# The chunk-gating stage of a hybrid diffusion step: b_s as a VectorE addend, and the scan's opening inside the gating rounds

## Chip, cores and metric

The kernel runs on one core of one Trainium2 chip. The metric is the device time of one execution in microseconds. Arithmetic is f32 throughout; a product of two f32 operands takes TensorE two records in the profile, and a transpose takes one.

## What is computed

One layer for 128 context tokens and 256 latent tokens (384 columns, three tiles of 128), model width 2048. The part that matters here is the middle of `token_mix`: the gating half (`y_g`), and what the scan needs first of each head pair (decay, `a`, `kk`, `kd`).

```python
za = za + p['mu_shift'] * (shift_fn(za) - za)
r, k, v, g = (za[..., i * D_A:(i + 1) * D_A] for i in range(4))
lw = za[..., 4 * D_A:4 * D_A + 2 * LORA_W].reshape(b, t, 2, LORA_W)
la = za[..., 4 * D_A + 2 * LORA_W:].reshape(b, t, 2, LORA_A)
wl = (p['w0'] + jnp.einsum('btdr,drc->btdc', jnp.tanh(lw), p['w2'])).astype(F32)
decay = jnp.exp(-jnp.exp(-jax.nn.softplus(-wl) - 0.5))
a = jax.nn.sigmoid((p['a0'] + jnp.einsum('btdr,drc->btdc', la, p['a2'])).astype(F32))
kk = (k * p['k_k']).astype(F32).reshape(b, t, H_A, HEAD_A)
kk = kk / jnp.maximum(jnp.linalg.norm(kk, axis=-1, keepdims=True), 1e-12)
kd = k.astype(F32)[:, :, None] * (1.0 + (a - 1.0) * p['k_a'].astype(F32))
...
u = jax.nn.gelu(zb[..., :D_B])
vg = layernorm(jax.nn.gelu(zb[..., D_B:]), p['ln_v_w'], p['ln_v_b'])
vc = vg.reshape(b, t // CHUNK, CHUNK, H_B, HEAD_B)
sp = jnp.einsum('hpq,bnqhc->bnphc', p['w_s'], vc) + p['b_s'].T[:, :, None]
y_g = u * sp.reshape(b, t, D_B)
```

`b_s` has one value per head and position in the chunk (8 x 128). It is the same for all 128 channels of a head and for the three chunks.

## The kernel before

Activations lie with channels on the 128 partitions and the 384 tokens along the free dimension: `z` holds one block of 128 channels per index, PSUM (`ps`) has eight banks. The program is a row of Blocks, each with one instruction list per engine; all engines meet at the end of a Block. In front of the change lie the modulation and the input projection (until about 533 us), behind it the scan (607 to 1168 us), the output projection and the expert mixer.

**The gating Block.** It first makes statistics: means of `vg` (TensorE into bank 0, VectorE subtracts), squares of the keys summed by head (bank 6), and the variance of `vg` (bank 1), from which ScalarE and VectorE make `rstd` by a square root and a reciprocal. Then come eight rounds (HB = PAIRS = 8), one for each head of the gate and one pair of key heads. All rings have two slots (RING = 2).

- TensorE, round j: `over_heads(j)` spreads the inverse key norms over the partitions (a matmul of 16 rows and 384 columns), `turn(j)` transposes three tiles of the normalised `vg`, and `mix(j - 1)` does, for each of three tiles, a matmul of one row that puts `b_s` into the bank (row of ones times `bsp`) and then the matmul with `w_s` on top. `mix(HB - 1)` follows the last round.
- ScalarE, round j: `affine(j + 1)` (weight and bias of the layer norm, into `vn`), `copy(j)` (the transposed tiles from PSUM to `vt`).
- VectorE, round j: `scale(j + 2)` (times `rstd`), `key(j + 1)` (writes `kk`), `gate(j)` (u times the mix, read from PSUM).
- SyncE loads `w_s`, `b_s` on one partition, the spreading matrix, and three of the modulation weights that the scan uses up later (1 MB each).

**The scan Block.** It has eight head pairs, one after another. Each starts from values that its opening makes: TensorE's four `front` matmuls (64 rows, 384 columns, from `lora`, the loaded w2 and a2 of the pair), ScalarE's `front_gates` (sigmoids) and `front_factors` (exponentials), and VectorE's 18 `front_step`s (prefix sums, centring, `kd` and the products bq and kq). For pairs 1 to 7 the opening is woven into the pair before; for pair 0 it stands at the head of the Block, ahead of everything else, and SyncE's load of `lora` for it as well. After the opening, TensorE transposes bq, kq and (when POOL has copied it) `vs`, VectorE makes the kr products, TensorE makes 12 score products into PSUM and VectorE masks them (L1065). POOL's list in this Block starts with clearing and filling `c32`, two copies of identities, and then the copy of `vs`. Order on each engine is that of the program; waits are on semaphores that count instructions.

Of the kernel before, what the change touches and what calls it, by code (L numbers as in the profile page):

```python
# [23 lines left out]
ALU = mybir.AluOpType  # L24
# [3 lines left out]
P = 128  # L28
# [21 lines left out]
RING = 2  # L50
# [109 lines left out]
def build_program(nc, x_t, c_t, cols_in, tables_in, spread_in, w_ada, w_in, w2a2, w_s, b_s, state_t, w_out, w_query,  # L160
# [9 lines left out]
    with ctx:  # L170
# [419 lines left out]
        ka1 = sb(g_scope, "ka1", [P, PAIRS])  # L590
        with ExitStack() as c_scope, nc.Block() as block:
            wsp = sb(c_scope, "wsp", [P, HB, P])
            bsp = sb(c_scope, "bsp", [1, HB, P])
# [9 lines left out]
            mixed, gated = sem("mixed"), sem("gated")  # L603
# [61 lines left out]
            def _(act):  # L665
                nc.scalar.activation(z[:, Z_LW, :], z[:, Z_LW, :], ACT.Tanh)
# [87 lines left out]
        with ExitStack() as d_scope, nc.Block() as block:  # L754
# [4 lines left out]
            lora = buf("lora", [P, 2, P])  # L759
# [3 lines left out]
            sg = [buf(f"sg{d}", [P, T]) for d in range(2)]  # L763
            aa = [buf(f"aa{d}", [P, T]) for d in range(2)]
            cum = buf("cum", [P, T])
            bon = buf("bon", [P, T])
            cen = [buf(f"cen{d}", [P, T]) for d in range(2)]
            cex = [buf(f"cex{d}", [P, T]) for d in range(2)]

            fac = [[sg[0], cex[0], buf("fac0", [P, T])], [sg[1], cen[1], buf("fac1", [P, T])]]  # L770
            tot = [buf(f"tot{d}", [P, TILES]) for d in range(2)]
            half_next = [buf(f"halfnext{d}", [P, TILES]) for d in range(2)]
            half = [buf(f"half{d}", [P, TILES]) for d in range(2)]
            half2 = [buf(f"halftwo{d}", [P, 1]) for d in range(2)]
            kd = [buf(f"kd{d}", [P, T]) for d in range(2)]
            bq = aa
            kq = [fac[0][2], fac[1][2]]

# [23 lines left out]
            def signal(name, per):  # L802
                return Signal(sem(name), per)

            y_copied, state_stored = sem("y_copied"), sem("state_stored")
            lora_landed, state_landed = sem("lora_landed"), sem("state_landed")
            v_copied, gates_in, gates = signal("v_copied", 1), signal("gates_in", 4), signal("gates", 4)
            centred, factors = signal("centred", 2), signal("factors", 2)
            multiplied = signal("multiplied", 4)
# [20 lines left out]
            front_chain = sem("front_chain")  # L830

            def zb(first, it):
                return z[:, bass.ds(it + first, 1), :].rearrange("p o t -> p (o t)")

            def colr(name, it, more=0):
                return cols[:, bass.ds(it + (COLS[name][0] + more), 1)]
# [23 lines left out]
            def _(sp):  # L860
# [24 lines left out]
                load_lora(0)  # L885
# [33 lines left out]
            def _(act):  # L919
                K = EXP_HALF  # L920

                def front_gates(it, d):
                    gates_in.wait(act, it, 2 * d + 1)
                    gates.inc(nc.scalar.activation(sg[d][:, :], ps[:, 6, 0:T], ACT.Sigmoid, bias=colr("w0", it, PAIRS * d)))
                    gates_in.wait(act, it, 2 * d + 2)
                    gates.inc(nc.scalar.activation(aa[d][:, :], ps[:, 7, 0:T], ACT.Sigmoid, bias=colr("a0", it, PAIRS * d)))

                def front_factors(it, d):
                    centred.wait(act, it, d + 1)
                    srcs = ((cen[d], -K), (cex[d], -K), (cen[d], K)) if d == 0 else ((cex[d], K), (cen[d], K), (cex[d], -K))  # L930
                    for i, (src, sc) in enumerate(srcs):
                        nc.scalar.activation(fac[d][i][:, :], src[:, :], ACT.Exp, scale=sc)
                    factors.inc(nc.scalar.activation(half_next[d][:, :], tot[d][:, :], ACT.Exp, scale=-K))

# [11 lines left out]
                def one(it, more):  # L946
# [9 lines left out]
                    if more:  # L956
                        operands.wait(act, it, 2)
                        halves.wait(act, it, 2)
                        front_gates(it + 1, 0)
                    for n in range(NL * GR):  # L960
# [5 lines left out]
                        if more:  # L966
                            if n == 0:
                                front_gates(it + 1, 1)
                                nc.scalar.activation(zb(Z_G, it), zb(Z_G, it), ACT.Sigmoid)
                            elif n in (7, 11):  # L970
                                front_factors(it + 1, n // 4 - 1)
# [25 lines left out]
            def _(dve):  # L997
                FRONT = 20

                def front_step(it, n):  # L1000

                    d = n // 4 if n < 8 else (n - 8) // 5
                    fc = Chain(dve, front_chain, it, FRONT)
                    if n < 8:
                        k = n % 4
                        fc.n = 7 * d + (0, 3, 4, 7)[k]
                        if k == 0:
                            gates.wait(dve, it, 2 * d + 1)
                            if d:
                                fc.wait(7)  # L1010
                            for i in range(TILES):
                                c = slice(i * P, (i + 1) * P)
                                fc.done(nc.vector.tensor_tensor_scan(cum[:, c], table("ones"), sg[d][:, c], 0.0, ALU.mult, ALU.add))
                        elif k == 1:
                            fc.wait()
                            fc.done(nc.vector.tensor_scalar(tot[d][:, :], cum[:, P - 1:T:P], 0.5, None, ALU.mult))
                        elif k == 2:
                            fc.wait()
                            for i in range(TILES):
# [1382 lines left out]
```

## Time and profile before

| | us |
|---|---|
| median of 3 runs | 3145.44 |
| lowest and highest | 3135.82 to 3153.9 |
| the profiled execution | 3150.04 |
| its span | 3148.3 |
| TensorE busy in the span | 2918.8 |
| VectorE, ScalarE, POOL busy | 2139.9, 1203.8, 874.3 |

The profile is of one execution. PE is TensorE's matmuls and PEld its weight loads, DVE is VectorE, ACT ScalarE, POOL GpSimd, SP SyncE. A timeline row tells start, duration, engine, line, operation, output and inputs, count of merged records, and in brackets how long the engine had been idle and who released it. The whole stage that the change touches is 2.4% of the span, and the opening of pair 0 another 0.5%, so the page of totals says little of them; stretches and timelines do. Matmul records overlap, so the pace of matmuls is the distance from start to start, not the duration.

### The profile page before, as it was taken

Reading aid. Unit: us, or ns where it says so; the run is one execution under the profiler, and the core shown is the slowest. Engines: PE = TensorE matmul, PEld = TensorE weight load, DVE = VectorE, ACT = ScalarE, POOL = GpSimd, SP = SyncE. Lnnn points to the kernel's source line nnn. Section 1 sums busy time; section 2 is a strip of 40 time slices with the busy share of each in tenths; the row PEclk is TensorE's granted clock in tenths of the full one; section 3 lists DMA queues with packets and bytes.
Section 4 is the critical chain, followed back from the end, with each engine's and each line's share of the span. In section 5 each row is a group of like instructions: output and inputs, shape, how many; then the busy total and the mean of one; then the engine's idle time right before and its main releaser. Section 6 shows DMA issues by size and latency. Waiting matters only on the chain.

```text
span 3148.3 us, 62824 instructions
## 1 busy us (share of the span) xinstructions
PE 2918.8 (93%) x25976; PEld 2621.9 (83%) x25976; DVE 2139.9 (68%) x3018; ACT 1203.8 (38%) x1773; POOL 874.3 (28%) x554
## 2 busy tenths in 40 slices
PE   6899999899999999969998999999997999999997
PEld 5799998477787778959998999999996887777776
DVE  1455532455565545368994988887776999989997
ACT  2433333233333333252334555454332433333333
POOL 0000000022222211026774444331112344343431
PEclk8899999599999998979998999999998999999998
DMA  9533333033443333235566999999999999999995
GB/s 386 206 131 120 133 122 113 4 113 126 139 155 125 128 127 118 80 135 196 198 230 240 361 394 396 388 332 398 412 383 392 418 418 418 417 418 418 418 417 239
DMA packets 207556, 815.23 MB, mean 259 GB/s; under 512 B 81505, under 2 KB 101089, under 8 KB 118274
## 3 DMA queue, kind: packets, MB, share of 16 engines
q1 hardware_dynamic: 104898, 527.19, 44.9%
q0 software_dynamic: 36864, 268.45, 20.5%
q10 hardware_dynamic: 65600, 16.78, 2.4%
q8 instruction: 149, 2.44, 0.3%
q14 instruction: 45, 0.37, 0.0%
HBM read 771.98 MB, written 40.37 MB: 258 GB/s over the span
## 4 chain that ended last, share of the span: by engine, by line
PE 27%; DMA 13%; DVE 8%; issue 3%; POOL 2%; ACT 1%; another core or an unknown queue 1%; SPq 1%; DVEq 0%; ACTq 0%; POOLq 0%
DMA work<-act_table 11%; PE ps L1697 6%; PE ps L1698 6%; PE ps L1699 6%; POOL wlo L1687 2%; DVE work L2282 2%; DVE x L2187 2%; PE ps L2044 1%; PE ps L2045 1%; PE ps L2046 1%; PE ps L1951 1%; PE ps L1953 1%; PE ps L1952 1%; DVE wlo L2287 1%; PE ps L2013 1%
## 5 line engine op out<-in xcount | busy, mean ns | idle before, releaser
L1697 PE MATMUL ps<-hhi,whi 128*128 128x256 f32 x2048 | 589.1, 288 | 19.4 <-POOL wlo L1687 10.6
L1698 PE MATMUL ps<-hlo,whi 128*128 128x256 f32 x2048 | 581.7, 284 | 0.0
L1699 PE MATMUL ps<-hhi,wlo 128*128 128x256 f32 x2048 | 581.6, 284 | 0.0
L2044 PE MATMUL ps<-whi,hhi 128*128 128x512 f32 x1024 | 402.3, 393 | 33.2 <-DVE hlo L2265 18.1
L1697 PEld LDWEIGHTS ps<-hhi,whi 128*128 128x128 f32 x2048 | 395.2, 193 | 24.3 <-POOL wlo L1687 13.1
L2077 POOL DMA_INDIRECT work<-expert_v,idx x128 | 289.7, 2263 | 442.0 <-DVE work L2282 420.0
L2045 PE MATMUL ps<-wlo,hhi 128*128 128x512 f32 x1024 | 399.7, 390 | 0.0
L2046 PE MATMUL ps<-whi,hlo 128*128 128x512 f32 x1024 | 399.3, 390 | 0.0
L1698 PEld LDWEIGHTS ps<-hlo,whi 128*128 128x128 f32 x2048 | 395.4, 193 | 0.0
L1699 PEld LDWEIGHTS ps<-hhi,wlo 128*128 128x128 f32 x2048 | 395.1, 193 | 0.0
L2077 POOL DMA_INDIRECT x<-u_rows,idx x128 | 231.8, 1811 | 471.2 <-DVE x L2187 275.6
L265 PE MATMUL ps<-hhi,whi 128*128 128x384 f32 x1040 | 349.9, 336 | 5.6 <-DVE hlo L357 5.6
L266 PE MATMUL ps<-hlo,whi 128*128 128x384 f32 x1040 | 348.3, 335 | 0.0
L267 PE MATMUL ps<-hhi,wlo 128*128 128x384 f32 x1040 | 348.2, 335 | 0.0
L2282 DVE SCALAR_TENSOR_TENSOR work<-work,dots 128x2048 f32<-128x2048 f32 x127 | 297.8, 2345 | 0.1
L1687 POOL TENSOR_TENSOR wlo<-raw,whi 128x2048 fp32r<-128x2048 f32 x40 | 200.0, 5003 | 264.2 <-ACT whi L1807 171.6
L2044 PEld LDWEIGHTS ps<-whi,hhi 128*128 128x128 f32 x1024 | 192.8, 188 | 82.6 <-DVE wlo L2287 24.7
L254 DVE TENSOR_TENSOR wlo<-raw,whi 128x2048 fp32r<-128x2048 f32 x66 | 150.9, 2288 | 152.0 <-ACT whi L248 152.0
L2187 DVE SCALAR_TENSOR_TENSOR x<-x,htok 128x2048 f32<-128x2048 f32 x88 | 226.9, 2584 | 6.4 <-DMA x<-u_rows,idx 5.9
L2046 PEld LDWEIGHTS ps<-whi,hlo 128*128 128x128 f32 x1024 | 192.8, 188 | 40.5
L2045 PEld LDWEIGHTS ps<-wlo,hhi 128*128 128x128 f32 x1024 | 192.8, 188 | 39.3
L1912 ACT ACTIVATE whi<-raw 128x2048 fp32r<-128x2048 f32 x64 | 122.9, 1921 | 222.5 <-PE ps L2046 212.7
(330 smaller groups left out, 5486.9 us busy)
## 6 DMA issues: line engine op xcount, KB each, us to landing
raw<-expert_u SPq DMA_DIRECT2D x94, 1024.0 KB, 7.2
x<-w_ada SPq DMA_DIRECT2D x64, 1024.0 KB, 5.3
work<-expert_v SPq DMA_DIRECT2D x64, 1024.0 KB, 14.7
raw<-expert_v SPq DMA_DIRECT2D x64, 1024.0 KB, 14.7
raw<-w_in SPq DMA_DIRECT2D x50, 1024.0 KB, 4.8
raw_more<-expert_u SPq DMA_DIRECT2D x34, 1024.0 KB, 8.4
z<-w_ada SPq DMA_DIRECT2D x32, 1024.0 KB, 14.0
raw<-w_out SPq DMA_DIRECT2D x16, 1024.0 KB, 4.8
```

The source lines that it names most:

```text
L265: pe.matmul(bank, hi[:, k, :], hhi[:, k, :], start=(k == 0), stop=False)
L266: pe.matmul(bank, hi[:, k, :], hlo[:, k, :], start=False, stop=False)
L267: last = pe.matmul(bank, lo[:, k, :], hhi[:, k, :], start=False, stop=(k == KD - 1))
L1697: pe.matmul(bank, whi[:, r, k, :], moving_hi, start=(k == 0), stop=False)
L1698: pe.matmul(bank, whi[:, r, k, :], moving_lo, start=False, stop=False)
L1699: last = pe.matmul(bank, wlo[:, r, k, :], moving_hi, start=False, stop=(k == KD - 1))
L2044: pe.matmul(bank, ah, vh[:, part], start=first, stop=False)
L2045: done = pe.matmul(bank, ah, vl[:, part], start=False, stop=False)
L2046: done = pe.matmul(bank, al, vh[:, part], start=False, stop=last)
L2077: nc.gpsimd.indirect_dma_start(out=buf, out_offset=None, in_=rows, in_offset=bass.IndirectOffsetOnAxis(ap=idx[:, s:s + 1], axis=0)).then_i ...
L2187: nc.vector.scalar_tensor_tensor(out=ug[s % UG], in0=ug[s % UG], scalar=1.0, in1=htok[:, :], op0=ALU.mult, op1=ALU.mult, accum_out=dots[:, ...
L2282: nc.vector.scalar_tensor_tensor(out=accs[:, :], in0=vg[n], scalar=dots[:, bass.ds(it * 4 + n, 1)], in1=accs[:, :], op0=ALU.mult, op1=ALU. ...
```

## The change

- `b_s` is loaded on all 128 partitions (`bsp` is [P, HB, P]). The matmuls of one row are gone from `mix`. VectorE has a new `add_bias(j)` that reads the mix from PSUM, adds `bsp` (the same for the three tiles) and writes a new buffer `biased` (two slots); `gate(j)` reads that. The bank is given back after `add_bias`.
- The opening of pair 0 leaves the head of the scan Block. `lora` is loaded in the gating Block, behind `spread`. TensorE runs front sums 0 and 1 around `over_heads(0)`, and sums 2 and 3 in rounds 1 and 2, all in banks 0 and 1. ScalarE runs the gates of direction 0 ahead of `affine(0)`, those of direction 1 after `copy(2)`, and the factors after `copy(3)` and `copy(4)`. VectorE runs steps 0 and 1 ahead of round 0 and the others between `add_bias` and `gate` of the eight rounds.
- The buffers and the helper functions move to the scope that both Blocks share; their bodies are the same but for the banks.

```diff
+        FRONT_IN_ROUND = ((2, 3), (4, 5), (6, 7), (8, 9, 10), (11, 12), (13, 14), (15, 16), (17,))
...
+        def front_sums(pe, it, n, banks=(6, 7)):
+            if n == 0:
+                pe.wait_ge(lora_landed.sem, it * 16 + 16)
+            if n >= 2:
+                gates.wait(pe, it, n - 1)
+            r = slice(64 * (n // 2), 64 * (n // 2) + 64)
+            gates_in.inc(pe.matmul(ps[:, banks[n % 2], 0:T], lora[r, n % 2, :], z[r, (Z_LW, Z_LA)[n % 2], :], start=True, stop=True))
...
-            bsp = sb(c_scope, "bsp", [1, HB, P])
+            bsp = sb(c_scope, "bsp", [P, HB, P])
+            biased = sb(c_scope, "biased", [P, RING, T])
...
-                sp.dma_start(bsp[:, :, :], b_s).then_inc(loads.sem, 16)
+                sp.dma_start(bsp[:, :, :], b_s.to_broadcast([P, HB, P])).then_inc(loads.sem, 16)
                 sp.dma_start(spread[:, :], spread_in).then_inc(loads.sem, 16)
+                sp.dma_start(lora[:, :, :], w2a2[0]).then_inc(lora_landed.sem, 16)
...
                     if j >= RING:
-                        pe.wait_ge(gated.sem, j - RING + 1)
+                        pe.wait_ge(bias_added.sem, j - RING + 1)
                     for c in range(TILES):
-                        out = ps[:, 4 + u, c * P:(c + 1) * P]
-                        pe.matmul(out, table("ones")[0:1, :], bsp[:, j, :], start=True, stop=False)
-                        last = pe.matmul(out, vt[:, u, c * P:(c + 1) * P], wsp[:, j, :], start=False, stop=True)
+                        last = pe.matmul(ps[:, 4 + u, c * P:(c + 1) * P], vt[:, u, c * P:(c + 1) * P], wsp[:, j, :],
+                                         start=True, stop=True)
...
+                pe.wait_ge(tanh_done.sem, tanh_done.v + 1)
+                front_sums(pe, 0, 0, (0, 1))
+                over_heads(0)
+                pe.wait_ge(act_to_dve.sem, act_to_dve.v + 1)
+                front_sums(pe, 0, 1, (0, 1))
                 for j in range(HB):
-                    over_heads(j)
+                    if j:
+                        over_heads(j)
                     turn(j)
+                    if j in (1, 2):
+                        front_sums(pe, 0, j + 1, (0, 1))
                     if j:
                         mix(j - 1)
                 mix(HB - 1)
...
+                front_gates(act, 0, 0, (0, 1))
                 affine(0)
                 for j in range(HB):
                     if j + 1 < HB:
                         affine(j + 1)
                     copy(j)
+                    if j == 2:
+                        front_gates(act, 0, 1, (0, 1))
+                    if j in (3, 4):
+                        front_factors(act, 0, j - 3)
...
+                def add_bias(j):
+                    dve.wait_ge(mixed.sem, j + 1)
+                    nc.vector.tensor_tensor(biased[:, j % RING, :].rearrange("p (c t) -> p c t", c=TILES),
+                                            ps[:, 4 + j % RING, 0:T].rearrange("p (c t) -> p c t", c=TILES),
+                                            bsp[:, j:j + 1, :].to_broadcast([P, TILES, P]), ALU.add).then_inc(bias_added.sem, 1)
+
                 def gate(j):
-                    dve.wait_ge(mixed.sem, j + 1)
-                    nc.vector.tensor_tensor(z[:, Z_U + j, :], z[:, Z_U + j, :], ps[:, 4 + j % RING, 0:T], ALU.mult).then_inc(gated.sem, 1)
+                    dve.wait_ge(bias_added.sem, j + 1)
+                    nc.vector.tensor_tensor(z[:, Z_U + j, :], z[:, Z_U + j, :], biased[:, j % RING, :], ALU.mult)
 
                 scale(0)
                 scale(1)
                 key(0)
+                dve.wait_ge(loads.sem, loads.v + 48)
+                for n in range(2):
+                    front_step(dve, 0, n)
                 for j in range(HB):
                     if j + 2 < HB:
                         scale(j + 2)
                     if j + 1 < HB:
                         key(j + 1)
+                    add_bias(j)
+                    for n in FRONT_IN_ROUND[j]:
+                        front_step(dve, 0, n)
                     gate(j)
...
-                load_lora(0)
...
-                for step in (front_gates, front_factors):
-                    for d in range(2):
-                        step(0, d)
...
-                for n in range(18):
-                    front_step(0, n)
...
-                for n in range(4):
-                    front(0, n)
```

## Rows read from the trace of the kernel before

**Rows 1.** Stretches: busy us (records) of the engines, granted clock, DMA share, GB/s

```profile
core 0: us, PE busy (x) PEld busy (x) DVE busy (x) ACT busy (x) POOL busy (x), PEclk, DMA share, GB/s
...
534.00:545.00 11.00, 11.00 (x35) 4.64 (x34) 3.55 (x5) 8.99 (x14) 0.00 (x0) 1.00 0.90 324
...
549.00:556.00 7.00, 3.25 (x9) 1.29 (x7) 4.57 (x5) 2.98 (x5) 0.00 (x0) 0.84 0.00 0
...
568.00:574.00 6.00, 6.00 (x17) 3.47 (x16) 1.64 (x3) 1.20 (x2) 0.00 (x0) 0.50 0.00 0
...
608.00:620.00 12.00, 5.72 (x11) 2.65 (x11) 7.87 (x23) 7.00 (x14) 3.33 (x4) 0.50 0.09 27
```

**Rows 2.** Timeline of one gating round, TensorE

```profile
568.25 1.64 PE L643 MATMUL ps<-inv,spread 16*128 16x384 f32 x2
...
569.82 0.90 PE L635 MATMUL ps<-tab,vn 128*128 128x128 f32 x3
...
570.65 0.79 PE L653 MATMUL ps<-bsp,scan_tab 1*128 1x128 f32 x2
...
571.38 0.80 PE L654 MATMUL ps<-wsp,vt 128*128 128x128 f32 x2
...
575.00 1.64 PE L643 MATMUL ps<-inv,spread 16*128 16x384 f32 x2
```

**Rows 3.** Timeline of the entry to the rounds

```profile
549.37 0.58 ACT L675 ACTIVATE rstd<-ps,eps 128x384 f32<-128x384 f32 x1 [4.41 <-PE ps L625]
549.98 2.55 DVE L708 RECIPROCAL rstd<-rstd 128x384 f32<-128x384 f32 x1 [2.06 <-ACT rstd L675]
...
553.92 0.90 PE L635 MATMUL ps<-tab,vn 128*128 128x128 f32 x3 [3.75 <-ACT vn L681]
```

**Rows 4.** Timeline of the end of the rounds and the opening of pair 0

```profile
606.43 0.55 DVE L721 TENSOR_TENSOR z<-z,ps 128x384 f32<-128x384 f32 x1 [3.79 <-PE ps L654]
...
607.33 1.28 ACT L924 ACT_TABLE_LOAD   x1 [9.09 <-PEq L591]
...
609.41 5.24 PE L1140 MATMUL ps<-z,lora 64*128 64x384 f32 x8 [3.02 <-DMA lora<-w2a]
...
610.82 0.50 POOL L899 COPY vs<-z 128x384 f32<-128x384 f32 x1
...
611.09 0.58 ACT L924 ACTIVATE sg<-ps,cols 128x384 f32<-128x384 f32 x1 [2.48 <-PE ps L1140]
611.71 1.05 DVE L1013 TENSOR_TENSOR_SCAN cum<-scan_tab,sg 128x128 f32<-128x128 f32 x3 [4.72 <-ACT sg L924]
...
621.61 0.56 DVE L1043 TENSOR_TENSOR fac<-kd,fac 128x384 f32<-128x384 f32 x1
...
623.13 0.85 PE L1169 MATMUL ps<-tab,vs 128*128 128x128 f32 x3
...
623.91 1.23 PE L1184 MATMUL ps<-kr,aa 64*128 64x256 f32 x4
...
625.81 7.56 DVE L1065 TENSOR_TENSOR G<-ps,scan_tab 128x512 f32<-128x512 f32 x12 [0.25 <-PE ps L1184]
```

**Rows 5.** Timeline: pairs of 128-row matmuls in pair 0; 16-row matmuls in a row

```profile
678.77 0.49 PE L1285 MATMUL ps<-s,kr 128*128 128x128 f32 x2
...
679.19 0.69 PE L1289 MATMUL ps<-vtok,G 128*64 128x64 f32 x16
...
682.10 0.39 PE L1312 MATMUL ps<-vtok,btok 128*128 128x128 f32 x2
...
682.32 0.39 PE L1311 MATMUL ps<-sa,btok 128*128 128x128 f32 x2
...
1182.75 9.29 PE L1444 MATMUL ps<-inv,spread 16*128 16x384 f32 x14 [3.33 <-DVE inv L1501]
```

**Rows 6.** Groups of VectorE's instructions, 549 to 607.2 us

```profile
L716 DVE SCALAR_TENSOR_TENSOR kk<-z,cols,ps 128x384 f32<-128x384 f32 x8 | 4.9, 613 | 5.6 <-PE ps L643 5.6
L721 DVE TENSOR_TENSOR z<-z,ps 128x384 f32<-128x384 f32 x8 | 4.4, 554 | 35.7 <-PE ps L654 35.7
L712 DVE TENSOR_TENSOR z<-z,rstd 128x384 f32<-128x384 f32 x8 | 4.3, 551 | 0.0
```

More of the change, by code:

```diff
@@ L590, in build_program @@
         ka1 = sb(g_scope, "ka1", [P, PAIRS])
+        lora = sb(g_scope, "lora", [P, 2, P])
+        sg = [sb(g_scope, f"sg{d}", [P, T]) for d in range(2)]
+        aa = [sb(g_scope, f"aa{d}", [P, T]) for d in range(2)]
+        cum = sb(g_scope, "cum", [P, T])
+        cen = [sb(g_scope, f"cen{d}", [P, T]) for d in range(2)]
+        cex = [sb(g_scope, f"cex{d}", [P, T]) for d in range(2)]
+        fac = [[sg[0], cex[0], sb(g_scope, "fac0", [P, T])], [sg[1], cen[1], sb(g_scope, "fac1", [P, T])]]
@@ new lines, in build_program, with signal @@
+        tot = [sb(g_scope, f"tot{d}", [P, TILES]) for d in range(2)]
+        half_next = [sb(g_scope, f"halfnext{d}", [P, TILES]) for d in range(2)]
+        kd = [sb(g_scope, f"kd{d}", [P, T]) for d in range(2)]
+        bq = aa
+        kq = [fac[0][2], fac[1][2]]
+        def signal(name, per):
+            return Signal(sem(name), per)
+        gates_in, gates = signal("gates_in", 4), signal("gates", 4)
+        centred, factors, multiplied = signal("centred", 2), signal("factors", 2), signal("multiplied", 4)
@@ new lines, in front_gates, with front_factors @@
+        def front_gates(act, it, d, banks=(6, 7)):
+            gates_in.wait(act, it, 2 * d + 1)
+            gates.inc(nc.scalar.activation(sg[d][:, :], ps[:, banks[0], 0:T], ACT.Sigmoid, bias=colr("w0", it, PAIRS * d)))
+            gates_in.wait(act, it, 2 * d + 2)
+            gates.inc(nc.scalar.activation(aa[d][:, :], ps[:, banks[1], 0:T], ACT.Sigmoid, bias=colr("a0", it, PAIRS * d)))
+        def front_factors(act, it, d):
+            centred.wait(act, it, d + 1)
+            srcs = ((cen[d], -EXP_HALF), (cex[d], -EXP_HALF), (cen[d], EXP_HALF)) if d == 0 else (
+                (cex[d], EXP_HALF), (cen[d], EXP_HALF), (cex[d], -EXP_HALF))
+            for i, (src, sc) in enumerate(srcs):
+                nc.scalar.activation(fac[d][i][:, :], src[:, :], ACT.Exp, scale=sc)
+            factors.inc(nc.scalar.activation(half_next[d][:, :], tot[d][:, :], ACT.Exp, scale=-EXP_HALF))
@@ new lines, in front_step @@
+        def front_step(dve, it, n):
+            d = n // 4 if n < 8 else (n - 8) // 5
+            fc = Chain(dve, front_chain, it, FRONT)
+            if n < 8:
+                k = n % 4
+                fc.n = 7 * d + (0, 3, 4, 7)[k]
+                if k == 0:
+                    gates.wait(dve, it, 2 * d + 1)
+                    if d:
+                        fc.wait(7)
+                    for i in range(TILES):
+                        c = slice(i * P, (i + 1) * P)
+                        fc.done(nc.vector.tensor_tensor_scan(cum[:, c], table("ones"), sg[d][:, c], 0.0, ALU.mult, ALU.add))
+                elif k == 1:
+                    fc.wait()
+                    fc.done(nc.vector.tensor_scalar(tot[d][:, :], cum[:, P - 1:T:P], 0.5, None, ALU.mult))
+                elif k == 2:
+                    fc.wait()
+                    for i in range(TILES):
+                        c = slice(i * P, (i + 1) * P)
+                        fc.done(nc.vector.tensor_scalar(cen[d][:, c], cum[:, c], tot[d][:, i:i + 1], None, ALU.subtract))
+                else:
+                    fc.wait()
+                    centred.inc(nc.vector.tensor_tensor(cex[d][:, :], cen[d][:, :], sg[d][:, :], ALU.subtract))
+            else:
+                k = (n - 8) % 5
+                fc.n = 14 + 3 * d + k
+                if k == 0:
+                    gates.wait(dve, it, 2 * d + 2)
+                    fc.done(nc.vector.tensor_scalar(kd[d][:, :], aa[d][:, :], colr("k_a", it), ka1[:, bass.ds(it, 1)], ALU.mult, ALU.add))
+                elif k == 1:
+                    fc.wait()
+                    fc.done(nc.vector.tensor_tensor(kd[d][:, :], kd[d][:, :], zb(Z_K, it), ALU.mult))
+                elif k == 2:
+                    fc.done(nc.vector.tensor_tensor(aa[d][:, :], kk[:, bass.ds(it, 1), :].rearrange("p o t -> p (o t)"),
+                                                    aa[d][:, :], ALU.mult))
+                elif k == 3:
+                    factors.wait(dve, it, d + 1)
+                    fc.wait()
+                    multiplied.inc(nc.vector.tensor_tensor(bq[d][:, :], aa[d][:, :], fac[d][2][:, :], ALU.mult))
+                else:
+                    multiplied.wait(dve, it, 2 * d + 1)
+                    multiplied.inc(nc.vector.tensor_tensor(kq[d][:, :], kd[d][:, :], fac[d][2][:, :], ALU.mult))
@@ L829, in build_program @@
                      state_out_ready, y_sum]
[L830 to L836, printed above, removed]
             def tiled(t):
@@ L919, in _ @@
             def _(act):
[L920 to L933, printed above, removed]
                 def ada_copy(it, slot):
@@ L1132, in _ @@
             def _(pe):
-                def front(it, n):
-                    if n == 0:
-                        pe.wait_ge(lora_landed.sem, it * 16 + 16)
-                    if n >= 2:
-                        gates.wait(pe, it, n - 1)
-                    r = slice(64 * (n // 2), 64 * (n // 2) + 64)
-                    gates_in.inc(pe.matmul(ps[:, 6 + n % 2, 0:T], lora[r, n % 2, :], z[r, (Z_LW, Z_LA)[n % 2], :], start=True, stop=True))
                 def ada(it, slot):
@@ L1201, in one @@
                     if more:
-                        front(it + 1, 0)
-                        front(it + 1, 1)
+                        front_sums(pe, it + 1, 0)
+                        front_sums(pe, it + 1, 1)
                     last_y = [None]
```

87 lines of the change are left out of this document (17 added, 70 removed).

## The prediction

> **What bounds the kernel now.** I looked first at the stretches of the gating stage and of the scan's first 30 us, with their granted clock; then at the timeline of one gating round; then at the two seams, into the rounds and out of them into the scan; last for places elsewhere in the trace with the same kinds of matmul. The stretches [rows 1] say two things. From about 554 us TensorE is granted 0.50, its lower level (1.2 GHz), and keeps it through all eight rounds, in which its records fill 6.00 of 6.00 us, while VectorE is busy 1.64 and ScalarE 1.20 of them. And between 608 and 620 us TensorE is busy only 5.72 of 12 us: the scan's first pair is being opened, and the pair's main work has not begun. So TensorE sets the pace of the rounds, and a chain TensorE, ScalarE, VectorE sets that of the opening.
>
> One round [rows 2] goes from over_heads at 568.25 to the next at 575.00: 6.75 us. In it over_heads takes 1.57, the three transposes of turn 0.83, and six pairs of records in mix 0.72 or 0.73 each, 4.35 us. Three of the six are the b_s matmuls of one row.
>
> At the entry [rows 3] TensorE sits idle for 3.75 us until 553.92, because VectorE's reciprocal of rstd ends only at 552.53 and the first scale and affine follow it. In this gap the clock falls. At the exit [rows 4] the last gate ends at 606.98 and the next block starts near 607.25 (ScalarE's table load at 607.33 is among its first instructions); the lora load holds TensorE till 609.41, VectorE's first scan starts at 611.71 and the last front product ends at 622.17, TensorE's score products start at 623.91 and VectorE's masks at 625.81. The masks are then VectorE's own 7.56 us.
>
> **The change, part by part.** *The b_s matmuls go.* 24 pairs of records at 0.72 us are 17.3 us on the engine that sets the pace. Is that all? Elsewhere, at half clock too, 14 back-to-back records of 16 rows and 384 columns take 9.29 us, about 0.64 each [rows 5]; 128 columns are then 0.21, and a pair of records 0.43. But a pair in mix takes 0.72: 0.29 is lost. Over_heads, two records of 0.64, takes 1.57 in the round: 0.29 lost again; turn, three of 0.21, takes 0.83: 0.19 lost. And in the scan at full clock pairs of 128 rows and columns that follow one another start 0.22 apart, while such a pair ahead of a matmul of 64 columns takes 0.42 [rows 5]. So what is lost is a change of the kind of matmul, not the pair. In a mix of only 128-row pairs I count 3 x 0.43 + 0.29 = 1.58 us, and turn, followed by its own kind, 0.64. A round is then 1.57 + 0.64 + 1.58 = 3.79 us in place of 6.75: 2.96 less, and 23.7 in eight. The two ends of this unknown: all gaps inside mix gone (this value), or every pair still 0.72 (17.3 saved). I take the first, since the nearest rows, L1311 and L1312, are the same shape in a row.
>
> The Trainium skill, TensorEngine Tiling (Array Packing), Key Properties, says that changing the tiling mode drains the engine; the trace's 0.72 against 0.43 agrees. By that rule the whole change is the 29 us of the sum below, and without it some 23.
>
> *Front sums move in.* Sums 0 and 1 run before the first turn. TensorE's three 384-column products there are some 1 us each even with gaps, inside the 3.75 us that it was idle. ScalarE adds a table load of 1.28 and two sigmoids of 0.58 [rows 4] after rstd is written at 549.95: done near 552.5, before affine(0) at about 553.1. Hidden; if the cover were gone, 2.4 us. Sums 2 and 3 lie in rounds 1 and 2: two records of 0.64, with 0.29 for the change of kind and 0.19 more for turn before it, 1.76 each, 3.5 us on the path.
>
> *VectorE's and ScalarE's rounds.* VectorE had scale 0.55, key 0.61, gate 0.55 [rows 6]; add_bias is a gate-like read of PSUM, 0.56 (bounds 0.5 to 0.7, since the spread b_s is one more SBUF operand). That is 2.27. The 18 front steps took 611.71 to 622.17, 10.46 us with waits, 1.3 a round. Mean 3.6 us, the round with three steps 2.27 + 3 x 0.55 = 3.9, against TensorE's 3.79. So VectorE all but fills the round; I charge 0.7 us in all. What does TensorE need from it? mix(j) needs the bank that add_bias(j - 2) freed, first in its round; turn needs scale and affine, done a round ahead; copy(j) stands behind affine(j + 1), and reaches mix with about 1.5 us to spare. ScalarE had 1.20 of 6 us and takes over part of the 7.00 that it had from 608 to 620, an Exp table load in round 3 among it: 2.9 us once, between copy(3) and affine(5), which eats that slack and no more. The step whose releaser is latest, the scan of d = 1 in round 1, needs the gates that ScalarE makes after copy(2); TensorE starts mix(1) after turn(2), so they are there by then.
>
> *The tail.* After mix(7) there were 0.11 us and one gate; now add_bias, step 17 and the gate: +1.2 us.
>
> *Queues.* SP issues one load more in this stage (lora, from the next block's queue) and b_s grows from 4 KB to 128 partitions of 4 KB, 0.5 MB. SP's queue is in order, so spread, lora and the three w_ada loads stand behind it. The 4 MB of the stage went at 324 GB/s by 545 [rows 1]; 0.6 MB more is 2 us, and the first reader waits until 549.3. POOL is passed by nothing. In the next block SP's first load of lora is gone and s_in is first.
>
> *The opening.* What is late next, when the fronts are done at the block's start? VectorE's kr products need 1.7 us. TensorE's transposes of vs need POOL's copy, which stands in its queue behind c32 and the identity copies and ended at 611.32 [rows 4], 4.07 after the block's start. From the transposes' start to the scores' was 0.78 (623.13 to 623.91). So scores start 4.85 after the block's start where it was 16.66: 11.8 saved. POOL's copies now run beside VectorE, and the clock may be at half for more of the score products, which then pass VectorE's 0.63 a mask only narrowly: 0.8 charged, bounds 0 to 3. Everything behind is a chain of blocks, so it moves up whole.
>
> **Sum.** -23.7 + 3.5 + 1.2 = -19.0 for the stage; -11.8 for the opening; +0.7 and +0.8: -29.0 us. Against the profiled execution's own 3150.0 us (span 3148.3) that is 3121.0; the median is 4.6 lower, so 3116.4, say 3117.
>
> **Rivals.**
> (a) *The gaps inside mix stay.* For it: in this stage no pair was seen without one. Against: rows 5. A pair costs 0.72, the stage saves 17.3 less 3.5 and 1.2, 12.6; with -11.8 and +1.5, -23: 3122.
> (b) *VectorE becomes the bound.* For it: five cross-engine waits a round, and 3.6 us of mean load in 3.79. Against: its waits are mostly for things long done. If each round were 4.4 us, 5 us more: -24: 3121.
> (c) *The clock does not stay at half.* TensorE's idle 3.75 us before 553.92 is partly filled with three products, and a round is denser in 128-row work. Against: the 14 records of 16 rows stood at half clock without a break [rows 5], and VectorE would then leave TensorE idle in each round. If it held full clock, VectorE would set the pace: about 3.1 to 3.9 a round from 557, end near 581 instead of 588: 8 us more, -37 to -38: 3108. The Trainium skill, TensorE: Matmul & The Clock Gate, Part 1, says that idleness brings the lower level and activity releases it; by that rule the filled gap gives this rival.
> (d) *The wide b_s load is slow* (the other sign). All 128 partitions read the same 4 KB of b_s, a pattern with no row in the trace; everything that over_heads needs is behind it in one queue. Hidden till 549.3, then 1 us for 1 us. It eats the whole gain at 578, and makes the kernel slower by over 0.5% from 594 on, that is if the load took 60 us. Against: 324 GB/s for its neighbours, and 0.5 MB would have to go at 9 GB/s.
> (e) *The change does not do what it says*, as that a step still waits in the next block: the fronts would have to be released there, and none of their signals is. Part of "same" below.
>
> **How the numbers follow.** Forecast 0.50, (a) 0.13, (b) 0.14, (c) 0.16, (d) 0.03, anything that keeps under half the gain 0.04. A measurement of this kernel tells no change from one within 0.5% (15.7 us; the runs before lie from 3135.8 to 3153.9). (a), (b), (c) and the forecast are all beyond it; with some noise around the first two, faster 0.89, same 0.08, slower 0.03. Range: from (c) with a few us of noise, 3104, to (a) with its bounds (3 us more at the opening, noise of 5), 3130; 0.8 of the mass and little more.
>
> **What would show it.** In the profile after: 128-row pairs in mix about 0.43 apart at granted clock 0.50 (0.72 if (a)); over_heads to over_heads 3.8 us in rounds 3 to 7 (4.6 if (a), with idle of TensorE for VectorE if (b), 3.3 at clock 1.00 if (c)); stage end about 19 us sooner; score products some 5 us after the block's start, released by POOL's vs copy; TensorE idle over 2 us before the first transposes still, not for loads. Wrong if VectorE's front steps hold back scale and so turn, if the first score products wait for kr, or if TensorE waits for b_s.

## The result, and the profile after

The changed kernel takes 3114.15 us (median of 6 runs, 3102.62 to 3121.96) beside 3143.66 us (6 runs) of the kernel before: ratio 0.9916, 95% interval 0.9893 to 0.9939, so 26 us less by the ratio (19 to 34 by the interval). The forecast was 3117, 28.4 us below the median known then. The profiled execution took 3102.62 us with a span of 3100.8, and is the shortest of the six; what it shows inside the gating stage and the opening is steady to 0.9 us from one profile to the next, what lies behind them is not (below).

Stretches of the changed kernel (busy us and records of each engine, granted clock, DMA share, GB/s), to set beside [rows 1]:

```profile
534.00:545.00 11.00, 11.00 (x35) 4.63 (x34) 5.12 (x6) 7.38 (x11) 0.00 (x0) 1.00 0.94 358
545.00:549.00 4.00, 4.00 (x13) 1.91 (x11) 1.93 (x2) 1.21 (x2) 0.00 (x0) 1.00 0.01 6
549.00:556.00 7.00, 4.92 (x14) 1.90 (x12) 5.60 (x10) 4.69 (x8) 0.00 (x0) 0.81 0.00 0
568.00:574.00 6.00, 6.00 (x21) 4.06 (x20) 5.44 (x13) 4.46 (x12) 0.00 (x0) 0.50 0.00 0
586.00:592.00 6.00, 3.20 (x15) 2.38 (x16) 5.88 (x8) 1.68 (x3) 4.39 (x5) 0.50 0.13 37
592.00:598.00 6.00, 5.66 (x38) 3.97 (x36) 4.36 (x7) 0.00 (x0) 1.11 (x2) 0.80 0.00 0
```

In the rounds (568 to 574) TensorE is still busy 6.00 of 6.00 us at granted clock 0.50, but VectorE has gone from 1.64 to 5.44 and ScalarE from 1.20 to 4.46: the opening has moved into idle time of these two. ScalarE's 4.46 holds its table load and the exponentials of both directions, which come only here; from 574.44 to 581.90 it is busy 2.05 of 7.46 us. The loads of the stage went at 358 GB/s and were over by 545.

One round of TensorE in the changed kernel's timeline, to set beside [rows 2]:

```profile
570.75 1.64 PE L741 MATMUL ps<-inv,spread 16*128 16x384 f32 x2
572.33 0.90 PE L733 MATMUL ps<-tab,vn 128*128 128x128 f32 x3
...
573.02 1.49 PE L750 MATMUL ps<-wsp,vt 128*128 128x128 f32 x6
...
574.44 1.00 PE L741 MATMUL ps<-inv,spread 16*128 16x384 f32 x1
```

The round is 3.69 us (570.75 to 574.44) instead of 6.75. Mix goes from 573.02 to 574.44, 1.42 us for its three pairs instead of 4.35 for six.

The first transposes, at the entry, to set beside [rows 3]:

```profile
552.32 0.55 PE L733 MATMUL ps<-tab,vn 128*128 128x128 f32 x3 [2.08 <-ACT vn L786]
```

The exit and the opening of pair 0 in the changed kernel's timeline, to set beside [rows 4]:

```profile
583.99 0.55 DVE L831 TENSOR_TENSOR biased<-ps,bsp 128x384 f32<-128x384 f32 x1
584.46 0.55 DVE L684 TENSOR_TENSOR fac<-kd,fac 128x384 f32<-128x384 f32 x1
584.92 0.55 DVE L837 TENSOR_TENSOR z<-z,biased 128x384 f32<-128x384 f32 x1
...
585.73 0.52 POOL L987 MEMSET c<- 128x512 f32 x1 [583.98 <-POOLq L686]
...
586.49 3.20 POOL L992 COPY z<-tab 128x1536 f32<-128x1536 f32 x2
586.50 1.86 DVE L1085 TENSOR_TENSOR kr<-z,sg 128x384 f32<-128x384 f32 x1
...
588.28 1.81 DVE L1081 SCALAR_TENSOR_TENSOR kr<-kk,cen 128x384 f32<-128x384 f32 x1
...
589.63 0.83 POOL L994 COPY vs<-z 128x384 f32<-128x384 f32 x1
...
590.51 0.90 PE L1188 MATMUL ps<-tab,vs 128*128 128x128 f32 x3 [2.80 <-POOL vs L994]
...
591.35 1.22 PE L1203 MATMUL ps<-kr,aa 64*128 64x256 f32 x4
591.37 0.62 DVE L1090 SCALAR_TENSOR_TENSOR bon<-kd,cols,z 128x384 f32<-128x384 f32 x1
...
593.46 7.75 DVE L1095 TENSOR_TENSOR G<-ps,scan_tab 128x512 f32<-128x512 f32 x12 [1.47 <-PE ps L1203]
```

The last gate ends at 585.47, POOL's first instruction of the scan Block starts at 585.73, the score products follow 5.62 us later, behind the transposes of vs that POOL's copy released (L1188), and the masks at 7.73. Before, these distances were 16.65 and 18.55 us.

For the comparison of kernels I take two distances from each profile: the *stage*, from the start of ScalarE's tanh to POOL's first instruction of the scan Block, and the *opening*, from there to the end of pair 0's masks. Three things limit what they say.

- The two profiles of the changed kernel differ by 0.9 us in the stage. In the first the clock fell at 553.4, in the second at 550.2, 1.9 us sooner when counted from the tanh, so more of its rounds 0 and 1 ran at 0.50. Differences of under 1 us in the stage say nothing.
- The scan behind the opening takes 535 to 543 us in the thirteen profiles although its code is the same. The four scans in which the clock did not fall took 535.0 to 537.2 us, the longest two, 541.7 and 543.3, had two falls.
- The Blocks behind the scan take 1963 to 1968 us in eleven profiles and 1979.5 and 1978.8 in two, that of the kernel before and that of the changed kernel without b_s. In each of these two one load of the expert mixer (gate_table) kept ScalarE waiting for 19.21 and 18.56 us, TensorE stood idle for 8.06 and 8.53 us, and the clock was at 0.50 for about 14 and 17 us; no other profile has such a pause there. Why the load was late no run says. Of the 47.4 us between the two profiled executions, 16.5 are this.

A single execution says little (six of the changed kernel spread over 19 us), so for the kernels that ran once only the stage and the opening count.

| | stage | opening | both, against before |
|---|---|---|---|
| before | 73.97 | 26.11 | |
| changed | 54.04 | 15.48 | -30.6 |
| changed, again | 54.94 | 15.80 | -29.3 |
| b_s half alone (two profiles) | 50.07, 50.07 | 26.83, 26.68 | -23.2, -23.3 |
| opening half alone | 77.59 | 15.83 | -6.7 |
| one-row matmuls as one | 64.48 | 26.65 | -9.0 |
| changed without b_s | 52.94 | 15.80 | -31.3 |
| changed, vs copied first | 54.94 | 13.74 | -31.4 |
| changed, gap filled | 48.66 | 15.53 | -35.9 |
| changed, wide over_heads | 48.61 | 15.93 | -35.5 |
| wide, vs first | 47.88 | 13.74 | -38.5 |
| wide, vs first, gap filled | 46.58 | 14.71 | -38.8 |

### The profile page after: what moved, and what is told of

Same layout as the page of the kernel before. It is cut to its first block, busy times and chain, and to the rows that moved or that the text cites. A ratio compares the mean times of both kernels' runs of the same rounds, so it can differ in the third digit from the quotient of the medians.

```text
span 3100.8 us, 62737 instructions
## 1 busy us (share of the span) xinstructions
PE 2891.5 (93%) x25928; PEld 2607.1 (84%) x25928; DVE 2145.5 (69%) x3026; ACT 1203.0 (39%) x1773; POOL 857.7 (28%) x554
## 4 chain that ended last, share of the span: by engine, by line
PE 27%; DMA 12%; DVE 9%; issue 4%; POOL 2%; ACT 1%; SPq 0%; DVEq 0%; ACTq 0%; POOLq 0%
DMA work<-act_table 10%; PE ps L1714 6%; PE ps L1716 6%; PE ps L1715 6%; DVE work L2299 2%; POOL wlo L1704 2%; DVE x L2204 2%; PE ps L2061 1%; PE ps L1968 1%; PE ps L2062 1%; PE ps L2063 1%; PE ps L1969 1%; PE ps L1970 1%; DVE wlo L2304 1%; PE ps L2030 1%
## 5 line engine op out<-in xcount | busy, mean ns | idle before, releaser
L1714 PE MATMUL ps<-hhi,whi 128*128 128x256 f32 x2048 | 588.1, 287 | 14.7 <-POOL wlo L1704 10.3
L2094 POOL DMA_INDIRECT work<-expert_v,idx x128 | 269.3, 2104 | 461.3 <-DVE work L2299 439.5
```

The lines of the kernel that those rows point to most:

```text
L1714: pe.matmul(bank, whi[:, r, k, :], moving_hi, start=(k == 0), stop=False)
L2094: nc.gpsimd.indirect_dma_start(out=buf, out_offset=None, in_=rows, in_offset=bass.IndirectOffsetOnAxis(ap=idx[:, s:s + 1], axis=0)).then_i ...
```

## The experiments

**The b_s half alone** (against the kernel before):

```diff
-                        pe.matmul(out, table("ones")[0:1, :], bsp[:, j, :], start=True, stop=False)
...
+                    add_bias(j)
                     gate(j)
```

> Only the b_s half: no one-row matmuls, add_bias on VectorE; the opening of pair 0 stays at the head of the scan. Theory (TensorE sets the round, and each change of matmul kind loses 0.29 us at half clock): rounds of 3.7 us in place of 6.75, tail +0.6, so the stage is 23 to 24 us shorter and the kernel about 3120; from the block's start to the first score products still 16.7 us. Rival (only the removed pairs count, 24 x 0.72): 17 us, 3126, rounds of 4.6. Second rival (the two halves help each other, VectorE's room in the round is what the opening uses): the half alone gives clearly less than 19 and the rest of the 29 needs both.

Measured 3111.95 us, ratio 0.9910 (0.9886 to 0.9933). Its TensorE in two rounds of the timeline:

```profile
568.32 1.64 PE L644 MATMUL ps<-inv,spread 16*128 16x384 f32 x2
569.90 0.90 PE L636 MATMUL ps<-tab,vn 128*128 128x128 f32 x3
570.59 1.49 PE L653 MATMUL ps<-wsp,vt 128*128 128x128 f32 x6
572.01 1.64 PE L644 MATMUL ps<-inv,spread 16*128 16x384 f32 x2
```

Rounds of 3.69 us (568.32 to 572.01), a stage 23.9 us shorter, an opening like that of before (26.83 against 26.11 us). So the pace of the changed kernel's rounds is there without the opening, and both rivals fall: the first (17 us, rounds of 4.6) and the second (clearly less than 19 from the half alone). The kernel's whole time, though, came out as low as that of the changed kernel, where the profiles put it 7 us above; this is taken up again below.

**The opening half alone** (against the changed kernel: b_s back in mix as one-row matmuls, the gate back on PSUM and ahead of the front steps):

```diff
+                        pe.matmul(out, table("ones")[0:1, :], bsp[:, j, :], start=True, stop=False)
...
-                    add_bias(j)
+                    gate(j)
                     for n in FRONT_IN_ROUND[j]:
                         front_step(dve, 0, n)
-                    gate(j)
```

> Only the opening half: the one-row matmuls stay in mix and the gate reads PSUM (it stands ahead of the round's front steps); front sums, gates, factors and steps of pair 0 run in the rounds. Theory: rounds 3 to 7 stay at 6.75 us, rounds 1 and 2 are 1.8 longer, the tail 0.6, the opening 11 shorter (score products 5.6 us after the block's start in place of 16.7): 7 us faster in all, 3137. Rival (the woven steps delay scale and turn in every round): rounds 3 to 7 over 7.2 us, and no gain.

Measured 3130.88 us (12 runs), ratio 0.9968 (0.9952 to 0.9985). Rounds 3 to 7 stay 6.75 us; the two with front sums take 8.32, 1.57 more. Stage +3.6, opening -10.3: 6.7 us. The median says more, 12.9 us; the interval (4.7 to 15) holds both. The woven steps delay nothing.

**The same columns with fewer changes of kind.** In the kernel before, one matmul of one row and 384 columns for the three of 128:

```diff
+                    pe.matmul(ps[:, 4 + u, 0:T].rearrange("p (c t) -> p c t", c=TILES), table("ones")[0:1, :],
+                              bsp[:, j:j + 1, :].to_broadcast([1, TILES, P]), start=True, stop=False)
...
-                        pe.matmul(out, table("ones")[0:1, :], bsp[:, j, :], start=True, stop=False)
...
```

> The kernel before, with the three one-row matmuls of a mix made one of 384 columns: the same columns pass through TensorE, but four changes of kind per round fewer. Theory (the loss sits at the change of kind): mix is 1.28 + 0.29 + 3 x 0.43 + 0.29 = 3.15 us in place of 4.35, the round 5.55, the stage 9.6 us shorter. Rival (every two-record pair costs 0.72 whatever its neighbour): mix 1.57 + 3 x 0.72 = 3.7, the round 6.1, 5 us. Third (only columns count): round unchanged, 6.75.

The timeline of one round:

```profile
558.96 1.64 PE L643 MATMUL ps<-inv,spread 16*128 16x384 f32 x2
560.53 0.90 PE L635 MATMUL ps<-tab,vn 128*128 128x128 f32 x3
561.36 1.64 PE L651 MATMUL ps<-bsp,scan_tab 1*128 1x384 f32 x2
562.94 1.65 PE L654 MATMUL ps<-wsp,vt 128*128 128x128 f32 x6
564.51 1.00 PE L643 MATMUL ps<-inv,spread 16*128 16x384 f32 x1
```

The round is 5.55 us (558.96 to 564.51) and mix 3.15 (561.36 to 564.51), both as the theory had it, and the stage is 9.5 us shorter with no column fewer. That settles what 0.72 us for a pair was: 0.43 of columns and 0.29 of changing between one row and 128. The Trainium skill, TensorEngine Tiling (Array Packing), Key Properties, says that a change of tiling mode drains TensorE; the loss fits that, but no run shows that one row beside 128 is such a change, and the price is this trace's. (3128.35 us, one execution.)

**The changed kernel without b_s** (the addition of b_s is left out; gate as in the opening half):

> The changed kernel without b_s at all (left out: the addition of b_s; the gate reads PSUM, ahead of the front steps). Theory (TensorE sets the rounds of the changed kernel and add_bias is hidden): rounds 3 to 5 stay 3.69 us, only the tail is about 1 us shorter. Rival (VectorE is the bound of the rounds): each round falls by up to 0.5 us, 4 us in all.

```diff
-                    add_bias(j)
+                    gate(j)
                     for n in FRONT_IN_ROUND[j]:
                         front_step(dve, 0, n)
-                    gate(j)
```

This kernel leaves out the addition, so it computes something else. Rounds stay 3.69 us, the stage is 1.1 us shorter (52.94 against 54.04, with the clock falling at 553.3 in both; 0.9 of it behind the last mix): add_bias costs its tail and nearly nothing else. VectorE was not the bound of the rounds. (3120.33 us, one execution, with the pause behind the scan told above.)

**The copy of vs first in POOL's list:**

```diff
+                v_copied.inc(nc.gpsimd.tensor_copy(vs[:, :], zb(Z_V, 0)))
                 nc.gpsimd.memset(c32[:, :, :], 0.0).then_inc(c32_ready.sem, 1)
...
-                    v_copied.inc(nc.gpsimd.tensor_copy(vs[:, :], zb(Z_V, it)))
+                    if it:
+                        v_copied.inc(nc.gpsimd.tensor_copy(vs[:, :], zb(Z_V, it)))
```

> The changed kernel with pair 0's copy of vs moved to the head of POOL's list, ahead of c32 and the identity copies. In the changed kernel the score products start 5.62 us after the block's start, held by that copy, and the masks 7.74 us after it; VectorE's kr, kd and bonus products end 6.3 us after it. Theory (the copy is what is late, but VectorE is next): scores about 3 us after the start, held by kr; masks at 6.3, 1.4 sooner, since VectorE must first finish its own. Rival (only the copy counts): masks 2.5 sooner. Second rival (TensorE at half clock is what is late): under 1 us, as the first scores stay slow.

Its opening in the timeline:

```profile
588.86 0.50 POOL L987 COPY vs<-z 128x384 f32<-128x384 f32 x1 [587.11 <-POOLq L686]
...
590.05 3.54 POOL L993 COPY z<-tab 128x1536 f32<-128x1536 f32 x2
...
590.46 1.81 DVE L1083 SCALAR_TENSOR_TENSOR kr<-kk,cen 128x384 f32<-128x384 f32 x1
...
591.39 1.07 PE L1205 MATMUL ps<-kr,aa 64*128 64x256 f32 x4
...
594.51 0.62 DVE L1092 SCALAR_TENSOR_TENSOR bon<-kd,cols,z 128x384 f32<-128x384 f32 x1
595.04 5.05 DVE L1097 TENSOR_TENSOR G<-ps,scan_tab 128x512 f32<-128x512 f32 x8
```

Scores start 2.53 us after the Block's start (588.86), the masks 6.18, right behind the bonus product and with no wait: 1.5 us sooner than in the changed kernel, as forecast, because VectorE is next. The opening is 1.7 us shorter. (3111.18 us, one execution.)

**The gap at the entry filled** with three products of 128 rows:

```diff
                 front_sums(pe, 0, 1, (0, 1))
+                for _ in range(3):
+                    pe.matmul(ps[:, 3, 0:T], table("mean_db"), wide[:, 0, :], start=True, stop=True)
                 for j in range(HB):
```

> The changed kernel with three more products of 128 rows and 384 columns (into a bank that nobody reads before it is written anew) between front sum 1 and the first turn, where TensorE is idle for 2.1 us. Theory 1 (rival (c) of the prediction: the idleness there is what brings the clock down, and without it the rounds would keep full clock): granted clock 1.00 through the first rounds, VectorE sets a round of about 3.3 us, the stage 3 to 5 us shorter. Theory 2 (the rounds themselves cannot hold the clock: 16-row products, transposes, waits): the clock falls one to three rounds later, or at once, the stage at most 1 us shorter, or longer by what the filling delays.

Stretches of it:

```profile
556.00:560.00 4.00, 4.00 (x17) 2.07 (x17) 3.63 (x9) 1.17 (x3) 0.00 (x0) 1.00 0.00 0
560.00:564.00 4.00, 2.52 (x16) 1.72 (x17) 3.55 (x11) 2.20 (x5) 0.00 (x0) 1.00 0.00 0
564.00:568.00 4.00, 2.48 (x12) 1.68 (x12) 3.93 (x9) 3.99 (x9) 0.00 (x0) 0.67 0.00 0
568.00:572.00 4.00, 4.00 (x15) 2.70 (x14) 3.97 (x9) 1.87 (x5) 0.00 (x0) 0.50 0.00 0
```

The clock stays at 1.00 past the entry, where it fell in the changed kernel, and comes down only at 565.4, when TensorE had been busy 2.5 of each 4 us, waiting for VectorE's rounds (3.93 of 4.00; ScalarE, with its table load and exponentials, 3.99). Both theories held a part: filling the idle time at the entry kept the clock up there, and the rounds then lose it themselves. The stage is 5.4 us shorter, more than theory 2 allowed. (3097.92 us, one execution.)

**over_heads with 128 rows** (112 of them zero):

```diff
-            spread = sb(c_scope, "spread", [16, PAIRS * P])
-            inv = sb(c_scope, "inv", [16, T])
+            spread = sb(c_scope, "spread", [P, PAIRS * P])
+            inv = sb(c_scope, "inv", [P, T])
...
+                nc.gpsimd.memset(spread[:, :], 0.0).then_inc(zeroed.sem, 1)
+                nc.gpsimd.memset(inv[:, :], 0.0).then_inc(zeroed.sem, 1)
```

> The changed kernel with over_heads as a product of 128 rows: spread and inv lie on 128 partitions, 112 of them zero (POOL clears them at the stage's start). The same columns pass through TensorE; what changes is the number of rows and that no change of kind is left in a round but those around the front sums. Theory: at half clock a round of TensorE is 1.28 + 0.64 + 1.28 = 3.2 us in place of 3.69, less than VectorE's, which then sets about 3.4; and since all rows work all the time, the clock should rise within the rounds, if rows count for it. Stage 3 to 5 us shorter, and the scores at the opening at full clock. Rival 1 (columns alone decide on the clock): 0.50 through the rounds, stage 2 us shorter. Rival 2 (the loss of 0.29 is not from rows): round stays 3.69.

Stretches of it:

```profile
552.00:556.00 4.00, 3.91 (x12) 2.12 (x13) 2.41 (x7) 2.21 (x5) 0.00 (x0) 0.63 0.00 0
556.00:560.00 4.00, 4.00 (x13) 2.48 (x12) 2.75 (x8) 0.07 (x1) 0.00 (x0) 0.52 0.00 0
560.00:564.00 4.00, 3.50 (x21) 2.30 (x19) 3.14 (x9) 2.02 (x5) 0.00 (x0) 1.00 0.00 0
564.00:568.00 4.00, 1.96 (x11) 1.28 (x11) 3.97 (x11) 3.97 (x8) 0.00 (x0) 1.00 0.00 0
```

The same columns, and the clock is back at 1.00 by 560, where in the changed kernel it stayed at 0.50 to the end of the stage. From 562 on VectorE is the one without idle time; ScalarE is as full only while its table load and exponentials last, to 570. Stage 5.4 us shorter. The edit changes two things at once, the rows of over_heads and, with them, the changes of kind around it, and no run tells which of the two the clock went by. The scores, contrary to the expectation, were at half clock again: TensorE waits 3.88 us for VectorE's tail and the Block's start, and the clock falls there a second time, at 580.4. (3102.33 us, one execution.)

**Wide over_heads and vs first:**

> The wide over_heads and the early vs copy together, in the changed kernel. Sum of the two if they are independent: 5 us below the changed kernel by their own stages (3 to 4 of the stage, 1.4 of the opening), so a ratio to the kernel before of about 0.989. Rival (VectorE already sets both places): under 2 us.

```diff
+            spread = sb(c_scope, "spread", [P, PAIRS * P])
+            inv = sb(c_scope, "inv", [P, T])
...
+                v_copied.inc(nc.gpsimd.tensor_copy(vs[:, :], zb(Z_V, 0)))
```

3100.35 us (5 runs, 3097.5 to 3101.7) against 3141.81: ratio 0.9874 (0.9854 to 0.9894). This is the version to keep: by stage and opening 38.5 us below before and 8 below the changed kernel (expected 5; the wide over_heads alone brought 5.4, not 3 to 4), by the ratios 40 and 13. The intervals touch (0.9894, and 0.9893 for the changed kernel); against the changed kernel's second measurement below (from 0.9900) they are apart. Its clock is not steady:

```profile
564.00:568.00 4.00, 2.64 (x11) 1.42 (x11) 3.97 (x11) 3.97 (x9) 0.00 (x0) 0.69 0.00 0
568.00:572.00 4.00, 3.91 (x15) 3.15 (x16) 3.93 (x9) 2.82 (x8) 0.00 (x0) 0.50 0.00 0
572.00:576.00 4.00, 3.69 (x24) 2.81 (x23) 3.97 (x10) 1.57 (x3) 0.00 (x0) 0.96 0.00 0
```

It fell in the rounds, at 565.5, and rose again at 572.3, which the same rounds did not do in the kernel above. The stage was no longer for it (47.88 against 48.61), since VectorE was the one without idle time at either level (3.93 to 3.97 of 4.00).

**All three together** (against wide over_heads and vs first):

```diff
+                for _ in range(3):
+                    pe.matmul(ps[:, 3, 0:T], table("mean_db"), wide[:, 0, :], start=True, stop=True)
```

> Wide over_heads, early vs copy and the three filling products in one kernel. VectorE sets the rounds at full clock with either of the first and the last, so they should not add up: if the clock now holds at 1.00 from the entry through all rounds, the stage is 1 to 2 us shorter than with the wide over_heads alone (48.3 to 48.6 us), by the two rounds with front sums. Rival (VectorE leaves TensorE so idle at full clock that it falls anyway): as e8, 48.3 us, and no faster.

```profile
564.00:568.00 4.00, 1.96 (x11) 1.28 (x11) 3.97 (x11) 3.56 (x6) 0.00 (x0) 1.00 0.00 0
```

The stage is 1.3 us shorter than without the filling (46.58), the clock holds at 1.00 through the rounds, and the opening is 1.0 longer, with the clock down in part of the scores and masks. 3105.18 us, ratio 0.9887 (0.9868 to 0.9907): nothing over wide over_heads and vs first. With VectorE as the bound (3.97 of 4.00) a faster TensorE buys little, and here the opening gave it back.

**The changed kernel and the b_s half side by side** (both unchanged, on one chip):

> The changed kernel once more, on the same chip as the b_s half alone. Stage and opening by the profiles: 30.6 us below the kernel before, 7.4 below the b_s half alone. Theory (both parts stand behind one another on the path, so the parts' gains add up): a median of 6 to 8 us below the b_s half. Rival (the opening's 7 us are given back somewhere behind, as the first medians, 3114 and 3112, would have it): equal medians.

> The b_s half alone once more, beside the changed kernel on the same chip: about 23 us below the kernel before by its stage and opening; theory 6 to 8 us above the changed kernel, rival the same.

3110.57 us (ratio 0.9921, 0.9900 to 0.9941) and 3120.24 us (0.9939, 0.9921 to 0.9957): the changed kernel is 9.7 us lower by the medians. The profiles say 6.0 for this pair and 7.4 for the first, up to the end of pair 0's masks. The rival (all of the opening's gain given back later) fits neither these medians nor the scans; but the intervals overlap, so by whole times alone the order is not settled. That a part is given back is not excluded: the scan behind the opening took 536.6 us on average in the four profiles with the old opening (535.4 to 538.4) and 539.1 in the nine with the new one (535.0 to 543.3). The ranges overlap, and all six scans of over 538 us have a fall of the clock in them, so this is no finding either.

## Why the prediction was right

*The price of the b_s matmuls* was right: the pair's 0.29 us is the change of kind, and it goes with the neighbour. Forecast -23.7 for the eight mixes; the b_s half alone took 23.9 off the stage with its longer tail counted (0.6), so about 24.5. The round was forecast at 3.79 and is 3.69. Part of the loss lies ahead of a change and part behind it: turn takes 0.69 for its 0.64 of columns, with the change ahead of it, and mix 1.42 for its 1.28, with the change behind it. Together that is 2.11, where the sum had 2.22, because it charged mix both parts and turn none.

*Front sums in rounds 1 and 2*: forecast 1.76 each; 1.57 in the opening half, where turn had a change behind it already, 1.87 in the changed kernel (557.82 to 563.38, less 3.69).

*VectorE*: forecast to fill the round nearly, at a mean of 3.6 us. It was busy 5.44 of 6 us, 3.0 to 3.4 in each of the rounds of 3.69, and never the bound, save in the tail: mix(7) follows mix(6) without an over_heads between, so that VectorE had add_bias(7) only at 583.99. From the start of TensorE's last record in mix to POOL's start it is 2.99 us, where it was 1.29 before and 1.87 in the b_s half: the tail grew by 1.7, forecast 1.2, and most of the 0.7 us of charge lay there. Tail (1.1) and the two front sums (3.7) are the 4.9 us by which the second profile's stage is longer than that of the b_s half; in the first it is 4.0, since part of its rounds 0 and 1 ran at clock 1.00. ScalarE was fuller than VectorE once: 3.66 of 3.69 us in the round of the table load (from 567.06), without lengthening it.

*The opening*: forecast 4.85 us to the scores and -11.8. It was 5.62 and -11.0: the right releaser, POOL's copy, but slower, ended 4.73 us after the Block's start where it was 4.06. The 0.8 us that the sum charged for this and for the clock is the size of what came, with -10.6 and -10.3 at the masks' end; the masks themselves took 7.76 and 8.08 us where they had taken 7.56.

*The sum*: -29.0 forecast, -30.6 and -29.3 in the two profiles, of which the stage has -19.9 and -19.0 (forecast -18.3 with its charge) and the opening the rest. By whole times it is -26 and -25, with intervals that hold the forecast. No large errors had to cancel.

*Rivals*: (a) and (b) are refuted by the b_s half, the one-row experiment and the kernel without b_s. (c) did not happen, but its mechanism is real, and one edit away: with 2 us of TensorE's gap filled it came in part. With the gap filled, over_heads wide and vs first, where the clock held through every round, the stage was 7.5 us shorter than the changed kernel's, near the 8 that (c) was priced at. (d) did not happen; the stage's loads, b_s on 128 partitions among them, went at 358 GB/s and were over 4 us ahead of their reader. The markers held, TensorE's idle time before the first transposes (2.08 us, forecast over 2) just so.

## What to carry to other kernels

A small matmul costs its columns plus the change from its neighbour's kind: before you move work off TensorE, look at which neighbours become alike, and if the work must stay, gather it by kind. Work that waits at the head of a stage can go into the idle time of the engines that do not set the stage before; then ask who is late next (here POOL's list, then VectorE), and read that from the first release after the seam. When a stage is set by a slow clock, see what TensorE did just before it fell: filling two microseconds, or giving a 16-row product all 128 rows with zeros, was worth more than 5 us each in the one execution that each had, until VectorE was the bound.

## What the runs showed of the hardware

- At granted clock 0.50 a change between 1-row or 16-row and 128-row matmuls costs 0.29 us. A group of three transposes between two changes loses 0.19 (turn, 0.83 for 0.64 of columns, before); with the change on one side only, turn loses 0.05 ahead of its columns and mix 0.14 behind them (0.69 for 0.64 and 1.42 for 1.28, the changed kernel).
- The same 384 columns with 128 rows instead of 16 went with a rise of the clock from 0.50 to 1.00 within two rounds, each time that it had fallen with them (down at 553.1 and up at 559.9 in wide over_heads; down at 565.5 and up at 572.3 in the wide kernel with vs first); with 16 rows it did not rise in eight. The changes of kind around over_heads went at the same time, so rows alone are not shown.
- The clock fell behind short pauses too: in the changed kernel behind one of 2.08 us, in the wide kernel with vs first at 565.5, with no pause of TensorE over 1.85 us in the 12 us before. The kernel with all three edits had the same pauses there and more behind them, and its clock stayed at 1.00 through the rounds.
- VectorE's kr products have two SBUF operands and took 1.86 and 1.81 us beside POOL's identity copies; before, when POOL was done with these, the same two took 0.56 and 0.55:

```profile
622.81 0.56 DVE L1055 TENSOR_TENSOR kr<-z,sg 128x384 f32<-128x384 f32 x1
623.29 0.55 DVE L1051 SCALAR_TENSOR_TENSOR kr<-kk,cen 128x384 f32<-128x384 f32 x1
```

  POOL's two copies went from 2.87 to 3.20. The Trainium skill, SBUF — State Buffer, section SBUF: two separate sides, says that the two engines hold one port pair by turns, each for a whole instruction, when VectorE has two SBUF inputs and GpSimd reads SBUF; the trace agrees. I had charged 0.8 us for it and the clock.
